# Expert items of 96 places instead of 128 in a two-layer decoder trunk

## The reference, cut to what matters

```
def swiglu(x, w1, w3, w2):
    return (jax.nn.silu(x @ w1) * (x @ w3)) @ w2

def moe_swiglu(h, router, w1, w3, w2):
    xt = h.reshape(B * T, D)                       # 256 x 1024
    logits = (xt @ router).astype(jnp.float32)     # 8 experts
    top_val, top_idx = lax.top_k(logits, TOP_K)    # TOP_K = 2
    gates = jax.nn.softmax(top_val, axis=-1)
    combine = sum over the two of one_hot(top_idx) * gates
    for e in range(N_EXPERTS):                     # w1, w3: 1024 x 3584, w2: 3584 x 1024
        out = out + combine[:, e:e + 1] * swiglu(xt, w1[e], w3[e], w2[e])
```

## Time and profile before

| | |
|---|---|
| three runs | 1585.7, 1589.42, 1591.21 us; median 1589.42 |
| profiled execution | span 1587.1 us from the first to the last instruction |
| outside the span in the profiled execution | not given apart from it; the median of the runs is 2.3 us above the span |
| TensorE busy | 1563.2 us (98% of the span) |
| VectorE, ScalarE busy | 1226.4 us (77%), 973.8 us (61%) |
| DMA | 470.75 MB, 297 GB/s over the span |
| granted TensorE clock | 0.997 of full |

### The profile page before, as it was taken

One profiled execution on the slowest core, in us unless ns is written; L12 is line 12 of the kernel. 1 busy time (PEld: TensorE's weight loads), 2 busy tenths in 40 slices (PEclk: granted clock), 3 DMA queues, 4 the chain that ended last, 5 costly groups with the idle time before them and its releaser, 6 DMA issues.

```text
span 1587.1 us, 24869 instructions
## 1 busy us (share of the span) xinstructions
PE 1563.2 (98%) x9653; PEld 1299.0 (82%) x9653; DVE 1226.4 (77%) x980; ACT 973.8 (61%) x815; POOL 68.4 (4%) x35
## 2 busy tenths in 40 slices
PE   9999899999999999999999999999999999999997
PEld 7778858888998888888888888888888888888885
DVE  7573657774764457989988988988988988988995
ACT  1522345554424456787777777777777777777774
POOL 0013600000000000020000000000000000000100
PEclk9999999999999999999999999999999999999999
DMA  9120269956445524999999999999999999999991
GB/s 316 62 86 23 83 240 356 338 186 227 160 170 189 202 113 176 401 416 381 403 390 357 395 403 349 391 400 351 389 390 359 393 387 360 397 386 358 403 412 66
DMA packets 78588, 470.75 MB, mean 297 GB/s; under 512 B 7860, under 2 KB 8244, under 8 KB 26932
## 3 DMA queue, kind: packets, MB, share of 16 engines
q1 hardware_dynamic: 67860, 442.13, 72.3%
q10 hardware_dynamic: 9504, 23.37, 3.9%
q0 software_dynamic: 1152, 4.19, 0.7%
HBM read 450.27 MB, written 19.40 MB: 296 GB/s over the span
## 4 chain that ended last, share of the span: by engine, by line
PE 96%; DVE 2%; ACT 1%; issue 1%; DMA 0%; DVEq 0%; SPq 0%; ACTq 0%
PE ps L1641 93%; PE ps L2219 2%; PE ps L2211 0%; DMA h<-x 0%; PE ps L1660 0%; DVE workr L1057 0%; PE ps L1879 0%; ACT work L887 0%; DVE work L1375 0%; DVE h L1615 0%; DVE small L1194 0%; ACT workr L725 0%; ACT pairs_r L732 0%; PE ps L1948 0%; PE ps L2082 0%
## 5 line engine op out<-in xcount | busy, mean ns | idle before, releaser
L1641 PE MATMUL ps<-pairs_r,workr 128*128 128x512 f32 x2856 | 661.8, 390 | 0.6 <-DVE workr L1383 0.6
L1641 PEld LDWEIGHTS ps<-pairs_r,workr 128*128 128x128 f32 x2856 | 534.8, 188 | 112.4 <-issue 1.1
L1641 PE MATMUL ps<-workr 128*128 128x512 f32 x2024 | 483.6, 393 | 0.0
L1641 PEld LDWEIGHTS ps<-workr 128*128 128x128 f32 x2024 | 375.6, 188 | 77.4 <-DVE workr L1610 0.4
L1547 DVE TENSOR_TENSOR workr<-ring,workr 128x2048 fp32r<-128x2048 f32 x167 | 380.6, 2289 | 51.7 <-ACT workr L969 51.6
L1547 DVE TENSOR_TENSOR pairs_r<-ring,pairs_r 128x2048 fp32r<-128x2048 f32 x165 | 373.9, 2288 | 19.3 <-ACT pairs_r L969 17.3
L969 ACT ACTIVATE pairs_r<-ring 128x2048 fp32r<-128x2048 f32 x165 | 316.6, 1920 | 111.1 <-PE ps L1641 101.9
L969 ACT ACTIVATE workr<-ring 128x2048 fp32r<-128x2048 f32 x167 | 319.2, 1917 | 42.4 <-PE ps L1641 35.7
L1094 DVE TENSOR_TENSOR pairs_r<-ring,pairs_r 128x2048 fp32r<-128x2048 f32 x68 | 155.8, 2291 | 110.5 <-ACT pairs_r L732 109.1
L1641 PE MATMUL ps<-mem 64*64 64x64 f32 (+6 forms) x3064 | 198.9, 263 | 9.6 <-issue 4.1
L732 ACT ACTIVATE pairs_r<-ring 128x2048 fp32r<-128x2048 f32 x65 | 124.4, 1914 | 124.7 <-PE ps L1641 121.6
(11 more groups left out here) (231 smaller groups left out, 646.3 us busy)
## 6 DMA issues: line engine op xcount, KB each, us to landing
ring<-mstream SPq DMA_DIRECT2D x336, 1024.0 KB, 7.2
ring<-pstream SPq DMA_DIRECT2D x65, 1024.0 KB, 4.9
mem<-rstream SPq DMA_DIRECT2D x27, 512.0 KB, 8.4
sent<-work ACTq DMA_DIRECT2D x6, 1024.0 KB, 8.3
back<-work ACTq DMA_DIRECT2D x6, 1024.0 KB, 11.7
mem<-rstream SPq DMA_DIRECT2D x16, 256.0 KB, 2.9
work<-sent ACTq DMA_DIRECT2D x7, 512.0 KB, 7.9
back<-work ACTq DMA_DIRECT2D x7, 512.0 KB, 9.2
```

Source lines behind the costliest of these rows:

```text
L1641: ins = nc.tensor.matmul(*args, **kw)
```

## The change

An item takes up to 96 tokens instead of 128 (`CAP = 96`), and up to five extra items are provided for instead of three (`EXTRA = 5`). The tiles of tokens are 96 wide: stationary operands of the expert matmuls have 128 rows and 96 columns, PSUM results lie on 96 partitions, the transposes give 96 columns, what is split out of PSUM after a transpose has 4 x 96 elements instead of 4 x 128 (`got4`), and 96 rows of `sent` and `back` are loaded and stored. An expert may now take up to two extra items (over 96 and over 192 tokens), so the table of extra items is worked out a little differently. The zero filling keeps its size: 1536 rows before (12 x 128) and now (`ROWS`).

```diff
+CAP = 96
-EXTRA = 3
+EXTRA = 5
+ROWS = 1536
...
-        xeTh, xeTl = (wk(a, 1024, "k s", workr, k=KT) for a in (5120, 6144))
+        xeTh, xeTl = (wk(a, KT * CAP, "k s", workr, k=KT) for a in (5120, 6144))
-        actTh, actTl = (wk(a, 1024, "b g s", workr, b=2, g=4) for a in (8192, 9216))
+        actTh, actTl = (wk(a, 8 * CAP, "b g s", workr, b=2, g=4) for a in (8192, 9216))
+        def got4(bank):
+            return ps[:, bank, :].rearrange("p (k s) -> p k s", k=4)[:, :, 0:CAP]
...  # ScalarE
-                act_f(ysb[:, 0:512], ps[:, 4, :], ACT.Copy)
-                act_f(ysb[:, 512:1024], ps[:, 5, :], ACT.Copy).then_inc(s_ye, 1)
+                act_f(ysb[0:CAP, 0:512], ps[0:CAP, 4, :], ACT.Copy)
+                act_f(ysb[0:CAP, 512:1024], ps[0:CAP, 5, :], ACT.Copy).then_inc(s_ye, 1)
-                a.dma_start(back[bass.ds(items * P, P), :], ysb).then_inc(s_yw, 16)
+                a.dma_start(back[bass.ds(items * CAP, CAP), :], ysb[0:CAP, :]).then_inc(s_yw, 16)
-                    act_f(actTh[:, i % 2], ps[:, 6 + i % 2, :].rearrange("p (g s) -> p g s", g=4),
-                          ACT.Copy).then_inc(s_ga, 1)
+                    act_f(actTh[:, i % 2], got4(6 + i % 2), ACT.Copy).then_inc(s_ga, 1)
-                        a.dma_start(xe, sent[bass.ds(e * P + P, P), :]).then_inc(s_xe, 16)
+                        a.dma_start(xe[0:CAP, :], sent[bass.ds(e * CAP + CAP, CAP), :]).then_inc(s_xe, 16)
-                    act_f(s1[:, j % 2, :], ps[:, 2 * (j % 2), :], ACT.Silu).then_inc(s_m1, 1)
+                    act_f(s1[0:CAP, j % 2, :], ps[0:CAP, 2 * (j % 2), :], ACT.Silu).then_inc(s_m1, 1)
...  # VectorE, before the first item's second half of tokens
-            link(V.tensor_scalar(over, ps[:, 6, 0:8], float(P), None, ALU.is_gt))
+            link(V.tensor_scalar(over, ps[:, 6, 0:8], float(CAP), None, ALU.is_gt))
+            link(V.scalar_tensor_tensor(out=over, in0=ps[:, 6, 0:8], scalar=float(2 * CAP), in1=over, op0=ALU.is_gt,
+                                        op1=ALU.add))
             link(V.tensor_tensor_scan(order, ones[:, 0:NE], over, 0.0, ALU.mult, ALU.add))
-            link(V.tensor_tensor(jump, order, eidx, ALU.subtract))
-            link(V.tensor_scalar(jump, jump, float(NE - 2), float(P), ALU.add, ALU.mult))
...  # rows(), inside the first item
+                link(V.tensor_tensor(before_, order, over, ALU.subtract))
+                link(V.tensor_tensor(jump, before_, eidx, ALU.subtract))
+                link(V.tensor_scalar(jump, jump, float(NE - 1), float(CAP), ALU.add, ALU.mult))
                 for n in range(EXTRA):
-                    ins = V.tensor_scalar(selx[:, n, :], order, float(n + 1), None, ALU.is_equal)
+                    ins = V.tensor_scalar(selx[:, n, :], before_, float(n), None, ALU.is_le)
                 for n in range(EXTRA):
-                    ins = V.tensor_tensor(selx[:, n, :], selx[:, n, :], over, ALU.mult)
+                    ins = V.scalar_tensor_tensor(out=selx[:, n, :], in0=order, scalar=float(n), in1=selx[:, n, :],
+                                                 op0=ALU.is_gt, op1=ALU.mult)
...  # VectorE in an item
-                    V.tensor_tensor(actTl[:, i % 2], ps[:, 6 + i % 2, :].rearrange("p (g s) -> p g s", g=4),
+                    V.tensor_tensor(actTl[:, i % 2], got4(6 + i % 2),
                                     actTh[:, i % 2].bitcast(F32), ALU.subtract).then_inc(s_gd, 1)
-                    V.tensor_tensor(act[:, j % 2, :], s1[:, j % 2, :], ps[:, 2 * (j % 2) + 1, :],
+                    V.tensor_tensor(act[0:CAP, j % 2, :], s1[0:CAP, j % 2, :], ps[0:CAP, 2 * (j % 2) + 1, :],
                                     ALU.mult).then_inc(s_ma, 1)
...  # TensorE
-                            ins = M(ps[:, 2 + g, q * P:(q + 1) * P], xn_[:, t, k * P:(k + 1) * P], oh[:, t, :],
+                            ins = M(ps[:, 2 + g, q * P:q * P + CAP], xn_[:, t, k * P:(k + 1) * P], oh[:, t, :],
                                     start=(t == 0), stop=(t == TT - 1))
-                            ins = M3(ps[:, 2 * (j % 2) + i, :], parts((xeTh, xeTl), k), parts(w, q),
+                            ins = M3(ps[0:CAP, 2 * (j % 2) + i, :], parts((xeTh, xeTl), k), parts(w, q),
                                      start=(k == 0), stop=(k == KT - 1))
-                            ins = nc.tensor.transpose(ps[:, 2 + g, q * P:(q + 1) * P], xe[:, k * P:(k + 1) * P], ident)
+                            ins = nc.tensor.transpose(ps[:, 2 + g, q * P:q * P + CAP], xe[0:CAP, k * P:(k + 1) * P],
+                                                      ident[0:CAP, 0:CAP])
-                        ins = nc.tensor.transpose(ps[:, 6 + i % 2, g * P:(g + 1) * P],
-                                                  act[:, i % 2, g * P:(g + 1) * P], ident)
+                        ins = nc.tensor.transpose(ps[:, 6 + i % 2, g * P:g * P + CAP],
+                                                  act[0:CAP, i % 2, g * P:(g + 1) * P], ident[0:CAP, 0:CAP])
-                                ins = M3(ps[:, 4 + c, :], parts((actTh, actTl), i % 2, 2 * half + g),
+                                ins = M3(ps[0:CAP, 4 + c, :], parts((actTh, actTl), i % 2, 2 * half + g),
```

More of the change, by code:

```diff
@@ L62 @@
 NI = NE + EXTRA
+ROWS = 1536
+assert ROWS >= (NI + 1) * CAP
 assert E_UNITS % RING == 0 and E_UNITS % M_PAIRS == 0
@@ L146, in build @@
         itab = sb("itab", 16, I32)
-        sent = nc.dram_tensor("sent", ((NI + 1) * P, D), F32, kind="Internal").ap()
-        back = nc.dram_tensor("back", ((NI + 1) * P, D), F32, kind="Internal").ap()
+        sent = nc.dram_tensor("sent", (ROWS, D), F32, kind="Internal").ap()
+        back = nc.dram_tensor("back", (ROWS, D), F32, kind="Internal").ap()
         ps = ctx.enter_context(nc.psum_tensor("ps", [P, 8, 512], F32))
@@ L271, in build @@
         nil = wk(24576, 512)
-        xeTh, xeTl = (wk(a, 1024, "k s", workr, k=KT) for a in (5120, 6144))
-        oh = wk(7168, 256, "t s", t=TT)
+        xeTh, xeTl = (wk(a, KT * CAP, "k s", workr, k=KT) for a in (5120, 6144))
+        oh = wk(7168, TT * CAP, "t s", t=TT)
         xe = wk(7168, 1024)
         yh, yl = (wk(a, 1024, base=workr) for a in (20480, 21504))
-        hot = wk(11264, 256, "t s", t=TT)
-        hot1 = wk(11520, 256, "t s", t=TT)
+        hot = wk(11264, TT * CAP, "t s", t=TT)
+        hot1 = wk(11520, TT * CAP, "t s", t=TT)
         hotT = wk(11776, 256, base=workr)
@@ L690, in _ @@
                 nc.gpsimd.indirect_dma_start(
-                    fetched[i], None, back, bass.IndirectOffsetOnAxis(itab[:, 8 + i:9 + i], 0)
+                    fetched[i], None, back, bass.IndirectOffsetOnAxis(itab[:, 10 + i:11 + i], 0)
                 ).then_inc(s_yl[i], 16)
@@ L1474, in _ @@
             gathered_low(0)
-            over, order, jump = rw(256, NE), rw(264, NE), rw(296, NE)
+            over, order, jump, before_ = rw(256, NE), rw(264, NE), rw(296, NE), rw(248, NE)
             past = rw(200, 16).rearrange("p (t e) -> p t e", t=TT)
             row = rw(216, 16).rearrange("p (t e) -> p t e", t=TT)
-            V.tensor_scalar(past, place, float(P), None, ALU.is_gt)
-            V.scalar_tensor_tensor(out=row, in0=eidx.unsqueeze(1).to_broadcast([P, TT, NE]), scalar=float(P), in1=place,
+            V.tensor_scalar(past, place, float(CAP), None, ALU.is_gt)
+            V.scalar_tensor_tensor(out=row, in0=eidx.unsqueeze(1).to_broadcast([P, TT, NE]), scalar=float(CAP), in1=place,
                                    op0=ALU.mult, op1=ALU.add)
             v.wait_ge(s_cum, 2)
-            link(V.tensor_scalar(over, ps[:, 6, 0:8], float(P), None, ALU.is_gt))
+            link(V.tensor_scalar(over, ps[:, 6, 0:8], float(CAP), None, ALU.is_gt))
+            link(V.scalar_tensor_tensor(out=over, in0=ps[:, 6, 0:8], scalar=float(2 * CAP), in1=over, op0=ALU.is_gt,
+                                        op1=ALU.add))
             link(V.tensor_tensor_scan(order, ones[:, 0:NE], over, 0.0, ALU.mult, ALU.add))
-            link(V.tensor_tensor(jump, order, eidx, ALU.subtract))
-            link(V.tensor_scalar(jump, jump, float(NE - 2), float(P), ALU.add, ALU.mult))
             gathered_low(1)
@@ L1495, in rows @@
                                      pick.rearrange("p (n t e) -> p n t e", n=2, e=NE), AX.X, ALU.add))
[L1496 to L1499 removed]
+                V.tensor_scalar(itab[:, 6:10], rw(232, 4), -1.0, None, ALU.add)
+                V.tensor_scalar(itab[:, 10:14], rw(232, 4), float(CAP - 1), None, ALU.add).then_inc(s_row, 1)
+                selx = rw(344, EXTRA * NE).rearrange("p (n e) -> p n e", n=EXTRA)
                 for n in range(EXTRA):
[L1501 removed]
+                    ins = V.tensor_scalar(selx[:, n, :], before_, float(n), None, ALU.is_le)
                 link(ins)
                 for n in range(EXTRA):
[L1504 removed]
+                    ins = V.scalar_tensor_tensor(out=selx[:, n, :], in0=order, scalar=float(n), in1=selx[:, n, :],
```

(15 more changed lines are left out.)

22 lines of the change are left out of this document (11 added, 11 removed).

## The result

The changed kernel takes 1597.49 us (median of 4 runs, 1595.77 to 1600.8) against 1589.01 us (4 runs, 1585.7 to 1591.21): a ratio of 1.0056 with a 95% interval of 1.0036 to 1.0075. It is slower by 8.5 us, where 7.6 us less was forecast. The profiled execution has a span of 1593.9 us.

The account below looks back on a forecast made before the run. TensorE, without idle time inside an item, was taken to bound the kernel. Transposes would save 7.6 us and all other terms 0, so 1589.4 - 7.6 = 1581.8 us, with a range from 1565 to 1592 us.

Parts of the forecast that it names:

- What bounds the kernel: Inside an expert item TensorE has no idle time; its matmuls and transposes set the 118.55 us, all else is cover.
- The number of items: The count of expert items stays at 8, since the fullest expert has 72 tokens and 96 places suffice.
- Part 1, the transposes: 280 transposes on the path stream 96 columns instead of 128, each 27 ns shorter: 7.6 us saved, bound 0.
- Part 2, the matmuls: 4032 expert matmuls still stream 512 columns; the shorter load is hidden: 0 saved, 56.9 us at the utmost.
- the 14.1 ns of unexplained time: What each expert matmul takes beyond streaming 512 columns: 227.4 ns against 213.3 ns, 56.9 us in all.
- Parts 3 to 5: PSUM copies, DMAs of 96 rows and routing all lie beside TensorE's work: 0 on the path.
- The drain between shapes: Rival: TensorE loses 0.14 us at each of 126 shape changes around transposes, 1599.4 us; 13% together with another loss.
- The rival of a load that frees the stream: Rival: the 14.1 ns of each expert matmul shrink with the columns loaded, 14.2 us more saved, 1567.6 us; 28%.
- The rule of the Trainium skill: Fast weight loads need 128 columns and not FP32; for the expert matmuls' loads, taken to leave the sum the same.

Follow-up runs that it names:

- e8: Changed kernel with tiles 512 bytes apart, matmuls loading all 128 columns, and 80 places per item instead of 96: 1583.16 us against 1590.65 for the kernel before.
- e7: Kernel before, with the expert matmuls loading only 32 of the 128 columns of each token tile: 1605.69 us in one run against 1590.65.
- e9: Kernel before, all 128 columns loaded, every token and activation tile 32 columns (128 bytes) further on in memory: 1611.47 us against 1589.47, ratio 1.0141.
- e1: Kernel before, with the expert matmuls loading 96 of the 128 columns of each token tile, tiles still 128 apart: 1599.42 us against 1589.65, ratio 1.0062.
- e2: Changed kernel with its token and activation tiles put 512 bytes apart again, 96 columns still loaded: 1590.74 us against 1589.65 for the kernel before, ratio 1.0005.
- e12: Kernel before, full width, all token and activation tiles 64 columns (256 bytes) further on in memory: 1587.17 us in one run beside 1586.43.

## Why the prediction was wrong, by its own steps

**What bounds the kernel** was right and carried through: TensorE without a gap, everything else cover, before and after. **The number of items** was right: `ring<-mstream` is issued 336 times after too.

**Part 1, the transposes,** was right in mechanism and in size: 0.33 us for four, 7.7 us by the rows where 7.6 were forecast. e8 confirms the reason, that the moving columns set the time.

**Part 2, the matmuls, is the step that failed**: "There a load a quarter as wide changes nothing. I take **0** from this". It measured 4.0 ns a matmul more, 16.2 us in all, twice the gain of part 1. The row that it leaned on was of plain f32 matmuls, whose stream is half as fast: 0.223 us for 256 columns, 0.87 ns a column, against 0.44 ns in the fp32r matmuls. It was the fp32r matmuls that the stationary operand's width and place disturbed; that the slower stream is what spares the others is not shown. The difference between the two kinds stood in the same part as the 14.1 ns of unexplained time, and should have warned that the row was no proxy. Worse than the value were the bounds: from 0 to a gain of 56.9 us. Nothing excluded a loss, and the text gave no reason against one; only the words "or another loss" beside the drains, 13% together, left it room. The one-sided bound put the upper end of the range at 1592 us. The estimate of the load's own duration was good (163 ns, measured 161) and beside the point.

The packing of the tiles was not costed at all. It stands in the diff as two lines on memory (`KT * CAP`, `8 * CAP`), and is a third of the loss.

**Parts 3 to 5** were right in that nothing of them is on the path. The 32 gathering matmuls kept their pace with 96 columns, 3.60 us from the first to the next work against 3.59. VectorE's low part takes 549 ns (estimate 580), VectorE has 103.66 us in an item (103.8).

**The rivals.** The drain between shapes did end on the right side, and its 1599.4 us came close to the 1597.49 measured, but that is luck: its mechanism is not there. A group of four transposes is at 0.33 us in full, and no added time lies beside it in the chain. What came in its place touches each matmul. The rival of a load that frees the stream fell with e7. The rule of the Trainium skill that only full tiles that are not FP32 get a fast load (TensorE: Matmul & The Clock Gate, Weight-path perf modes) was set aside because 128 columns lay on one line with narrower ones. The load of 96 columns, at 161 ns, is on that line too, so the durations still show no fast load that was lost; and e9 needs no such rule, since there all 128 columns are loaded, and the matmul is slower than with 96.

**What stays open.** That the width costs 2.7 ns at 96 columns, with every tile on a multiple of 256 bytes, is shown by e1 and e2; why is not. The durations of the loads lie in one line with their columns and the cost does not. That the load's reads and the stream's reads get in each other's way is only argued: it fits that an address matters and that the plain f32 rows showed nothing, but no run changed the stream's side. Nor was the width of the load separated from the width of the result in PSUM, which the matmul ties together.

## What to carry to other kernels

When TensorE has no gap, a shorter stationary operand buys nothing by itself, since its load is hidden; look at the time of a long run of matmuls in the chain, not at the load's duration. Shorten what is streamed (here the identity of a transpose) and, for fp32r matmuls of 512 columns as here, leave the stationary tile full and on a multiple of 256 bytes: here that split of the change is worth 14 us, 1583.3 against 1597.49. When no row shows the thing that is changed, bound its cost on both sides, and ask of the nearest row whether it is limited by the same thing.

## What the runs showed of the hardware

- An fp32r matmul of 512 moving columns, at the full clock and on average over the 72 between two groups of transposes, took 227.4 ns with a stationary tile of 128 columns that begins on a multiple of 256 bytes, and 233.3 ns with the same tile 128 bytes further on (e9); 256 bytes further on it was 227.2 ns (e12).
- With tiles that begin well, stationary widths of 124, 112, 96, 64 and 32 columns gave on average 227.6, 231.3, 230.1, 230.1 and 231.7 ns. With 112 columns it was 229.2 or 233.3 ns, by turns from one group of transposes to the next.
- A transpose of f32 took 109, 83 and 70 ns with 128, 96 and 80 moving columns; its stationary operand kept 128 columns throughout.
- The cost is uneven: with all tiles 128 bytes off (e9) the matmuls began alternately about 229 and 237 ns apart, where the kernel before had 226 or 227.
